# Norm factors behind the products, a half-size Fourier mix, and a gather in rounded passes

## What is computed

```python
# first block, two layers; both parts of a layer are gated residuals
hx = rmsnorm(x, g) * (1 + scale) + shift       # scale, shift, gate from silu(c) @ ada_w
x  = x + g1 * mixer(hx)        # layer 0: fft2(ortho) over tokens and 256-wide groups,
                               #          real part, @ w_o + b_o;  layer 1: RWKV scan
x  = x + g2 * ec_moe(hx)       # 16 experts, each takes its top 64 tokens (32 of context)
x  = rmsnorm(x, final_g)
# second block, two layers
h  = rmsnorm_2(x, norm_mix_g)                  # x * rsqrt(mean(x*x) + 1e-6) * g
p  = h @ w_in                                  # split: gmlp, ssd, and the latents c_q, c_kv, k_rope
x  = x + concat(gmlp, ssd, mla(rmsnorm_2(c_q) @ w_qb, rmsnorm_2(c_kv) @ w_kvb, k_rope)) @ w_out
x  = x + square(relu(rmsnorm_2(x, norm_mlp_g) @ w1)) @ w2
x  = rmsnorm_2(x, final_norm_g)                # at the end
```

## Time and profile before

| | us |
|---|---|
| median of 3 runs | 4090.1 |
| lowest, highest | 4081.94, 4090.91 |
| the profiled execution | 4094.43 |
| its span, first to last instruction | 4092.6 |
| TensorE busy in it | 3697.3 |
| DVE, ACT busy | 1310.9, 1017.0 |

### The profile page before, as it was taken

The page is one execution under the profiler, slowest core; times in us unless marked ns, Lnnn a source line. Parts: engine busy times, 40 slices in busy tenths (PEclk is TensorE's granted clock), DMA queues, the critical chain, the costliest instruction groups (busy, mean ns, idle before and its releaser), DMA issues.

```text
span 4092.6 us, 63317 instructions
## 1 busy us (share of the span) xinstructions
PE 3697.3 (90%) x28370; PEld 2279.9 (56%) x28370; DVE 1310.9 (32%) x2368; ACT 1017.0 (25%) x1974; POOL 260.6 (6%) x232
## 2 busy tenths in 40 slices
PE   6998999999799989998867887879989998998998
PEld 3556443433357678888352332235548884656886
DVE  2123000000443167776330000025433333444342
ACT  3012011111143155454110000114322221423231
POOL 0000000000000144433000000000000000000000
PEclk9987999999889999999979999989999999999999
DMA  8345889898035244332429999901222322112320
GB/s 292 103 139 173 306 307 362 313 351 294 0 141 183 65 112 92 68 83 77 141 103 381 375 375 387 351 23 48 71 62 93 93 83 77 48 52 78 98 97 21
DMA packets 530928, 666.74 MB, mean 163 GB/s; under 512 B 156553, under 2 KB 299145, under 8 KB 530657
## 3 DMA queue, kind: packets, MB, share of 16 engines
q1 hardware_dynamic: 520544, 633.40, 45.8%
q10 hardware_dynamic: 6912, 18.88, 1.2%
q0 software_dynamic: 3200, 10.42, 0.7%
HBM read 631.18 MB, written 31.46 MB: 162 GB/s over the span
## 4 chain that ended last, share of the span: by engine, by line
PE 76%; DVE 8%; DMA 5%; SPq 4%; ACT 3%; POOL 3%; issue 1%; DVEq 0%; ACTq 0%; POOLq 0%
PE ps L657 12%; PE ps L662 4%; DMA ring<-in_moe_wu 4%; SPq L2710 4%; PE ps L520 3%; PE ps L850 3%; PE ps L2571 3%; PE ps L2572 3%; PE ps L2573 3%; PE ps L2587 3%; PE ps L2588 3%; PE ps L2586 3%; PE ps L823 3%; PE ps L2207 3%; PE ps L2313 3%; POOL ring L1403 3%
## 5 line engine op out<-in xcount | busy, mean ns | idle before, releaser
L657 PE MATMUL ps<-ring,H 128*64 128x512 f32 x2048 | 494.2, 601 | 52.1 <-DMA ring<-in_moe_wu 39.2
L657 PEld LDWEIGHTS ps<-ring,H 128*64 128x64 f32 x2048 | 147.3, 137 | 343.0 <-issue 252.4
L759 DVE TENSOR_TENSOR scr<-ps,scr 128x512 f32<-128x512 f32 x32 | 22.1, 692 | 965.5 <-PE ps L662 516.9
L657 PE MATMUL ps<-ring,scr 128*64 128x512 f32 x1024 | 248.3, 599 | 40.3 <-DMA ring<-in_moe_wd 38.8
L2571 PE MATMUL ps<-scr_rounded,ring_rounded 128*128 128x512 f32 x512 | 204.8, 400 | 23.0 <-ACT scr_rounded L2609 23.0
L2640 DVE TENSOR_TENSOR ring_rounded<-ring,scr_rounded 128x2048 fp32r<-128x2048 f32 x64 | 146.7, 2293 | 227.6 <-ACT scr_rounded L2606 227.5
L2572 PE MATMUL ps<-H_rounded,scr_rounded 128*128 128x512 f32 x512 | 204.6, 400 | 0.0
L2573 PE MATMUL ps<-scr_rounded 128*128 128x512 f32 x512 | 204.3, 399 | 0.0
L2588 PE MATMUL ps<-scr_rounded 128*128 128x512 f32 x512 | 202.5, 395 | 0.0
L2586 PE MATMUL ps<-scr_rounded,ring_rounded 128*128 128x512 f32 x512 | 201.8, 394 | 0.0
L2606 ACT ACTIVATE scr_rounded<-ring 128x2048 fp32r<-128x2048 f32 x64 | 122.1, 1907 | 257.7 <-PE ps L2588 246.4
(11 more groups left out here) (403 smaller groups left out, 6123.9 us busy)
## 6 DMA issues: line engine op xcount, KB each, us to landing
ring<-in_moe_wg SPq DMA_DIRECT2D x128, 1024.0 KB, 9.5
ring<-in_moe_wu SPq DMA_DIRECT2D x128, 1024.0 KB, 8.6
ring<-in_moe_wd SPq DMA_DIRECT2D x128, 1024.0 KB, 10.3
ring<-in_mlp_w SPq DMA_DIRECT2D x64, 1024.0 KB, 5.5
ring<-in_ada_w SPq DMA_DIRECT2D x48, 1024.0 KB, 7.4
ring<-in_w_in SPq DMA_DIRECT2D x14, 1024.0 KB, 5.2
ring<-in_w_out SPq DMA_DIRECT2D x8, 1024.0 KB, 5.1
st_kka<-scr ACTq DMA_DIRECT2D x16, 384.0 KB, 3.5
```

What stands on the lines that cost most here:

```text
L657: ins = pe.matmul(bx[64 * n:64 * n + 64, :], stat_x(k), w[:, k % 4, :], start=k == 0, stop=k == KT - 1)
```

## The change

Three parts.

1. *Fourier mix.* The spectrum of real input is symmetric, so the first stage makes 129 cosines and 127 sines per group, 256 columns instead of 512. The second stage makes one tile per group instead of two, and one more tile per segment for the middle cosine of each group (`fh`, from ZH, four of 128 columns filled). The other half of H is the tile read backwards, and its row 0 comes from `fh`. The rows of `fnet_wo` are put in the mirrored order on the host.
2. *Gather.* For gathers 1 to 3 of the first mixture the tokens HT are split into a rounded part (ACT) and a rest (DVE), and each fp32 product becomes two rounded ones. Gather 0 and those of the second mixture stay.
3. *Norm factors.* For `n20` (with the final norm of the first block folded in), `n21`, `n30` and `n31` the products take H = X * gain, without the factor, as each tile is ready. The squares go to scratch, and the ones product follows the first product tile. The factor is applied later: in the latents through their own norm, to kr, and to H (and X) behind the latents for the other projections; in the MLP, where the factor leaves relu squared as its square, on the results before they are added to X. The splits of H and of the first two weight slots of the MLP move into the output projection. `phase` no longer waits in these stages. The output goes in four transfers.

```diff
@@ phase
-            if e != "G" and name[:3] in ("mla", "mix"):
+            if e != "G" and (name[:3] in ("mla", "mix", "wou", "mlp") or name[:2] in ("n2", "n3") or name == "moe1"):
@@ residual_scalar
+            if norm in SQUARES:
+                for m in tiles:
+                    if later(act, f"{tag}.x{m}"):
+                        act.wait_ge(*at(f"{tag}.x{m}"))
+                    for n, sq in enumerate(SQUARES[norm]):
+                        scale = col("final_g", m) if n else 1.0
+                        did(A_, act.activation(sq[:, m, :], X[:, m, 0:TX], ACT.Square, scale=scale).then_inc(scalar_done, 1))
+                    marks[f"{norm}.sq{m}"] = (A_, count[A_])
+                    if norm in HIGH:
+                        if later(act, f"{norm}.u{m}"):
+                            act.wait_ge(*at(f"{norm}.u{m}"))
+                        did(A_, act.activation(HHI[:, m, :], H[:, m, 0:TX], ACT.Copy).then_inc(scalar_done, 1), f"{HIGH[norm]}hh{m}")
+                        if m == 4:
+                            high_weights(act, int(norm[2]), 0)
+                        if m == 5:
+                            high_weights(act, int(norm[2]), 1)
+                return
@@ residual_vector
+                    if scale is not None:
+                        dve.wait_ge(*own(dve, V))
+                        did(V, dve.tensor_tensor(scale[1], t, scale[0], ALU.mult).then_inc(vector_done, 1), f"free.{tag}.{m}.{s0}")
+                        dve.wait_ge(*own(dve, V))
+                        did(V, dve.tensor_tensor(x, scale[1], x, ALU.add).then_inc(vector_done, 1))
+                        continue
...
                 marks[f"{tag}.x{m}"] = (V, count[V])
+                if norm in SQUARES:
+                    scaled_vector(dve, norm, m)
+                    if norm in HIGH and m == 6:
+                        low_weights(dve, int(norm[2]), 0)
+                    if norm in HIGH and m:
+                        low_vector(dve, norm, m - 1)
                 if norm in EARLY and m >= 2:
                     norm_sum(dve, norm, m - 1, w)
+            if KT - 1 in tiles and norm in HIGH:
+                low_vector(dve, norm, KT - 1)
@@ fnet_tensor
+                for gg in range(2):
+                    b = bank(pe, f"f1.{tt}.{gg}")
+                    for g in (2 * gg, 2 * gg + 1):
+                        o = 256 * (g % 2)
+                        for k in range(2):
...
+                            ins = pe.matmul(b[:, o:o + 256], H[:, 2 * g + k, tt * P:tt * P + P], DFT_C[:, k, :], start=k == 0, stop=k == 1)
...
+                b = bank(pe, f"fh.{s0}")
+                for n, tt in enumerate(tts):
+                    ins = pe.matmul(b[:, 0:sn], ZH[:, tt, :], table_of(n, 0), start=n == 0, stop=n == len(tts) - 1)
...
+                            ins = pe.matmul(b[:, 0:sn], Z[:, tt, g, cs * P:cs * P + P], table_of(n, cs),
@@ fnet_vector (groups 0 and 2; ACT takes 1 and 3)
+                    did(V, dve.tensor_copy(H[:, 2 * g + 1, s0 + 1:s0 + sn], t[:, sn - 1:0:-1]).then_inc(vector_done, 1))
+                    did(V, dve.tensor_copy(H[:, 2 * g + 1, s0:s0 + 1], t[:, 0:1]).then_inc(vector_done, 1))
+                    did(V, dve.tensor_copy(H[:, 2 * g, s0:s0 + sn], t[:, 0:sn]).then_inc(vector_done, 1), f"free.f2.{g}.{s0}")
...
+                    did(V, dve.tensor_copy(H[0:1, 2 * g + 1, s0:s0 + sn], YH[1 if s0 else 0][32 * g:32 * g + 1, :]).then_inc(vector_done, 1))
@@ gather(q)
+                if i == 0 and q:
...
+                                pe.matmul(b[:, lo:lo + w], HTL[:, tt, o], GM_r[:, tt, 0:w], start=tt == tts[0], stop=False)
+                                ins = pe.matmul(b[:, lo:lo + w], HTH[tt][:, o], GM_r[:, tt, 0:w], start=False, stop=tt == tts[-1])
@@ mla_tensor
+            latent("cq", 0, f"{t0}cq.0", 0)
+            sums_tensor(pe, hk)
+            latent("cq", 1, f"{t0}cq.0", P)
+            latent("cq", 2, f"{t0}cq.1", 0)
+            latent("ckv", 0, f"{t0}ckv", 0)
+            latent_norm("cq", 3)
+            latent("ckv", 1, f"{t0}ckv", P)
+            latent("kr", "", f"{t0}kr", 0)
+            latent_norm("ckv", 2)
@@ mla_vector (ahead of the query tiles)
+            variance("cq", 384, 0)
+            normed("cq", 3, 0, CQ, "qg")
+            variance("ckv", 256, 1)
...
+            did(V, dve.tensor_tensor(KW, t, RMS, ALU.mult).then_inc(vector_done, 1), f"free.{t0}kr")
...
+            for k in range(KT):
+                did(V, dve.tensor_tensor(H[:, k, 0:TX], H[:, k, 0:TX], RMS, ALU.mult).then_inc(vector_done, 1), f"{hk}.h{k}")
+            for k in range(KT) if l == 0 else ():
+                did(V, dve.scalar_tensor_tensor(X[:, k, 0:TX], X[:, k, 0:TX], col("final_g", k), RMS1, ALU.mult, ALU.mult).then_inc(vector_done, 1))
@@ mlp_vector
+            low_weights(dve, l, 1)
+            mean_vector(dve, f"n3{l}", MSQ)
+            did(V, dve.reciprocal(MSQ, MSQ).then_inc(vector_done, 1))
@@ end of sync
+            for k in range(0, KT, 2):
+                if later(sp, f"end.h{k + 1}"):
+                    sp.wait_ge(*at(f"end.h{k + 1}"))
+                did("out", sp.dma_start(out.rearrange("(k p) t -> p k t", p=P)[:, k:k + 2], H[:, k:k + 2, 0:TX]).then_inc(output_out, 16), by=16)
```

More of the change, by code:

```diff
@@ L378, in norm_sum @@
                 dve.wait_ge(*at(f"{norm}.sq0"))
+            if norm in SQUARES:
+                for sq in SQUARES[norm]:
+                    did(V, dve.tensor_tensor(sq[:, 0, :], sq[:, 0, :], sq[:, k, :], ALU.add).then_inc(vector_done, 1))
+                dve.wait_ge(*own(dve, V))
+                if k == KT - 1:
+                    marks[f"{norm}.sum"] = (V, count[V])
+                return
             did(V, dve.tensor_tensor(H[:, 0, 0:w], H[:, 0, 0:w], H[:, k, 0:w], ALU.add).then_inc(vector_done, 1))
@@ L590, in fnet_scalar @@
-            for b in range(ADA_F2[0], ADA_FO[1]):
+                        t = tile(act, f"f2.{g}.{s0}")
+                        did(A_, act.activation(H[:, 2 * g + 1, s0 + 1:s0 + sn], t[:, sn - 1:0:-1], ACT.Copy).then_inc(scalar_done, 1))
+                        did(A_, act.activation(H[:, 2 * g + 1, s0:s0 + 1], t[:, 0:1], ACT.Copy).then_inc(scalar_done, 1))
+                        did(A_, act.activation(H[:, 2 * g, s0:s0 + sn], t[:, 0:sn], ACT.Copy).then_inc(scalar_done, 1), f"free.f2.{g}.{s0}")
@@ L591, in fnet_scalar @@
+                        act.wait_ge(*own(act, A_))
+                        did(A_, act.activation(H[0:1, 2 * g + 1, s0:s0 + sn], y[32 * g:32 * g + 1, :], ACT.Copy).then_inc(scalar_done, 1))
+                        if s0 == 0:
+                            marks[f"fy.{2 * g}"] = marks[f"fy.{2 * g + 1}"] = (A_, count[A_])
+                    ada_scalar(act, ADA_F2[0] + (0 if s0 else 4) + g)
+            for b in range(*ADA_FO):
                 ada_scalar(act, b)
         def fnet_vector(dve):
+            did(V, dve.memset(Z[:, :, :, P:P + 1].rearrange("p t g c -> p (t g) c"), 0.0).then_inc(vector_done, 1))
@@ L618, in build @@
         GM = S(19200, 6, 256)
+        GM_r = S(19200, 6, 256, of=scr_r)
+        HTL = S(0, 6, D, of=scr_r)
+        HTH = [S(10240 + D * tt if tt < 4 else 16384 + D * (tt - 4), D, of=scr_r) for tt in range(6)]
         WORK = scr[0:NE, 19200:19200 + TA]
@@ L735, in out @@
                     marks[f"free.dc{i}.{e}"] = (A_, count[A_])
+            for tt in range(6) if i == 0 else ():
+                if later(act, f"xs{i}.0.{KT - 1}"):
+                    act.wait_ge(*at(f"xs{i}.0.{KT - 1}"))
+                did(A_, act.activation(HTH[tt], HT[:, tt, :], ACT.Copy).then_inc(scalar_done, 1), f"hth{tt}")
             for e in range(NE):
@@ L755, in experts_vector @@
                     onehot(e // 4 + 1)
+                for tt in range(6) if i == 0 and e == 0 else ():
+                    if later(dve, f"hth{tt}"):
+                        dve.wait_ge(*at(f"hth{tt}"))
+                    did(V, dve.tensor_tensor(HTL[:, tt, :], HT[:, tt, :], HTH[tt].bitcast(F32), ALU.subtract).then_inc(vector_done, 1), "htl" if tt == 5 else None)
                 t = tile(dve, f"ux{i}.{e}")
@@ L1918, in build @@
         MIX = S(0, KT, TX)
+        MEAN, RMS, MEAN1, RMS1 = (MIX[:, n, :] for n in range(4))
         CQ = S(4096, 3, TX)
@@ L2062, in mla_scalar @@
                     marks[f"free.{t0}{nm}{m}"] = (A_, count[A_])
-            for nm, n, c in (("cq", 384, 0), ("ckv", 256, 1)):
-                t = tile(act, f"{t0}s{nm}")
-                did(A_, act.activation(RC[:, c, :], t, ACT.Abs_reciprocal_sqrt, bias=eps[:, 0:1], scale=1.0 / n).then_inc(scalar_done, 1), f"free.{t0}s{nm}")
+            if later(act, f"{hk}.mean"):
+                act.wait_ge(*at(f"{hk}.mean"))
+            did(A_, act.activation(RMS, MEAN, ACT.Abs_reciprocal_sqrt).then_inc(scalar_done, 1))
+            if l == 0:
+                did(A_, act.activation(RMS1, MEAN1, ACT.Abs_reciprocal_sqrt).then_inc(scalar_done, 1))
+            marks[f"{hk}.rms"] = (A_, count[A_])
+            root("ckv", 256, 1)
```

296 lines of the change are left out of this document (176 added, 120 removed).

## The result

The changed kernel takes 3936.5 us (median; 3933.5 to 3939.8), the one before 4086.5 beside it: ratio 0.9633, 95% interval 0.9617 to 0.9650. The forecast was 3940, counted from the 4090.1 of before. Two profiled executions: 4094.4 before, 3935.8 after. The profiled one of before lies 8 us over its median, so the traces differ by 158.9 us and the medians by 150.0. (Another execution of before, further down, has a span of 4085.3 us. Three stages are shorter in it, by 6.4, 3.4 and 3.2 us, with less time at the lower clock; others are longer, and 7.3 us are left.)

The account below looks back on a forecast made before the run. The prediction took TensorE's queue and the gaps in it as the bound. Savings of 51.1, 16.8 and 82.2 us sum to 150.1, taken from the median 4090.1: forecast 3940 us, own range 3928 to 3952 (0.62).

Parts of the forecast that it names:

- part 1: Fourier mix: fewer and shorter fp32 products save 51.1 us, bounds 47 and 53.
- part 2: Gathers 1 to 3 of the first mixture in two rounded passes: save 17 us, range -10 to 23.
- part 3: Norm factors applied behind the products, with the output in four transfers: save 82.2 us in sum.
- The first stage: Fourier mix: 48 products of 512 columns become 48 of 256, saving 20.7 us.
- The first boundary: Second mixture to layer 0's first score: saves 29.3 us, with 4.4 already lost to DVE's queue.
- The MLP norms: Both layers, ahead of the MLP: 15.1 us of gap plus 2.7 of clock less 0.9, 16.9 each, twice 33.8.
- Layer 1's norm: Second layer's norm ahead of its latents: first score at 3467.6 instead of 3483.30, saving 15.7 us.
- The end: Output in four transfers as pairs of tiles are ready: end moves from 4092.6 to about 4089.2, 3.4 us.
- (a): Rival: DVE or ACT late behind the removed norms, 3 to 8 us per boundary; 3952 to 3975; chance with (d) 0.20.
- (d): Rival: the wait for the eighth input stands behind the sums, gaps only shrink to 3 to 5 us; with (a) 0.20.
- (b): Rival: rounded gather gains nothing, its short products waiting for loads or the clock falling; 3957 or 3967; chance 0.10.
- (c): Rival: MLP weight split becomes the bound at 7 us more DVE work per slot; slower than before, 4100; chance 0.01.

Follow-up runs that it names:

- before_again: The kernel before, unchanged, run once more for its low-clock stretches; 4087.1 us.
- after_again: The changed kernel, unchanged, run once more as the base for the others on this chip; 3937.9 us, ratio to before 0.9632.
- moe1_round: Changed kernel with gathers 1 to 3 of the second mixture in rounded passes as well; whole program 3923.1 us.
- x_late: Changed kernel with DVE scaling X behind layer 0's attention instead of ahead of the query tiles; first latent to first score 72.96 us against 77.17.
- out_one: Changed kernel with the output in one 2 MB transfer behind all eight scalings; last stage 378.29 us against 374.06.
- dve_more: Changed kernel with two (layer 0) or three (layer 1) idle DVE reciprocals ahead of each MLP weight split; layer 0 373.25 us against 359.64, layer 1 470.70 against 374.06.

## Why the prediction was right, and where it was not

**The sum.** 150.1 predicted, 150.0 between the medians. That close a hit is luck, as its terms show: part 1 was 3 us too high in its stage and some 3 us more are given back at the clock; part 2 was 4 to 7 us too low; part 3 was 82.2 and measured 83.5 in the traces (29.0 + 0.7 + 15.5 + 12.5 + 5.2 + 15.5 + 5.1), 84 by the ratios. The errors cancel. What held is the mechanism of each part.

**Part 1.** The second stage was right: context tiles 6.05 us (20.39 to 14.34) against 6.1, token tiles 24.0 (61.52 to 37.48) against 24.3. The first stage was mis-sized: 18.0 instead of 20.7. Of the 2.7 us, 0.9 are the wait for the last copies at the turn, which I hadn't looked for: I counted cover behind the last tile of the second stage and not behind the last of the first, where the new row `fh` wants every copy at once. Another 1.3 are the lower clock at the start: before, it cost 12 records 1.4 us more than later ones (6.73 against 5.3); after, 8 records 1.8 and a modulation block 0.9. But this belongs to the executions and not to the change. The clock rose 2.9 us behind the first product in the one of before and 5.8 in the one of after; in `before_again` and `after_again` it rose 4.3 and 4.4 us behind it, and the whole stage took 137.97 and 88.51 us, 49.5 less. The part was then 1.6 too high, 0.9 of it the wait.

**Part 2.** The terms: the eight products of 256 columns take 1.01 us of a tile, 0.126 each (seven at 0.12, one at 0.17), where I took 0.130; the four of 128 columns 0.10 each in the mean where I took 0.108; a tile 1.40 instead of 1.47 and a gather 11.25 instead of 11.8. From the old 17.49 that is 6.2, not 5.6. So 0.126 lies at the low end of the bounds I had worked out, 0.125 to 0.130, and I took the high end; without narrow products between them (the gathers of `moe1_round`) it is 0.12. The figures of the Trainium skill (TensorE: Matmul & The Clock Gate, LDWEIGHTS and Back-to-back issue gap) made a tile 1.30, below what came; the 0.11 of three of the four narrow ones agrees with its 107 ns for a load, the 0.06 of the fourth doesn't. What no term held are the 5 us at the clock. I priced a shorter product and never asked whether the clock's dips, which the trace of before holds too, would stay.

**Part 3.** The first boundary: 29.7 against 29.3 (its two instants, 2803.48 and about 2774.0, make 29.5, and the 110 records of latents and sums at 0.434 make 47.7 and not 47.2), and DVE's queue ahead of the query tiles, 4.4 us late by my count, is the 4.2 that `x_late` takes away. The MLP norms: 15.5 us at the boundary (15.1) and 1.8 in the MLP's first slots. Layer 1's norm: 15.9 (12.5 and 5.2, less 1.8) against 15.7. The end: 3.3 (5.1 less 1.8) against 3.4, and `out_one` shows that the four transfers carry it.

**The rivals.** (a) and (d) didn't occur: no boundary keeps a gap, and the ones product stands in the queue without a wait. (b) the opposite came: records of 256 columns stand 0.12 apart, with their loads. (c) didn't decide, but was misjudged: I took one chain of 4.2 us for all slots, where in a slot of the first product DVE has 2.6 us of other work beside the 2.3 of the split, and in the last ones of the second the residual tiles. By `dve_more` the slack was about 6.3 us in the first kind.

## What to carry to other kernels

A norm whose factor can be taken behind the product needs only its gain ahead of it: here each such boundary gave back its wait, 15 to 29 us, once the splits and squares stood beside the products before. A stage that waits for its transfers is not thereby free: a long run of products without a freed slot in it stops the queue, and shortening three by 6 us each paid 6.0, 3.9 and 0.6. And work that another engine does in front of what TensorE waits for should be asked who wants it first; the eight scalings of X were wanted 200 us later, by the next residual.

## What the runs showed of the hardware that I had not expected

The granted clock follows what ran before in ways that repeat. With fp32 gathers four executions of four have a clock of 0.97 in the last 126 us of experts, always behind products on 16 rows, and with rounded gathers seven of ten have 1.00, though the last gather ends over 100 us ahead of the first dip and the experts' instructions are the same. The other three, which have one dip, are those with the short stretch in front of the router. The cause is open: no run changed the 16-row products themselves. The same products in front of the router took 1.93 or 1.07 us a block, 7 us in all, in executions of one kernel.

Two rounded products of 256 columns cost 0.12 us each, against 0.217 for each of the two records of an fp32 product, and 0.233 for a rounded one of 512. At 128 columns one in four starts after 0.06 us, the others after 0.11, and the second wide product behind four narrow ones starts after 0.17 instead of 0.12.
